# Two-layer conditioned trunk: the conditioning products in plain fp32 with weights stationary, and in a new order

## The reference

```
shift, scale, gate = split(silu(c) @ w_ada + b_ada, 3)        # w_ada: 1024 x 3072, per layer
h = rms_norm(x, norm_g) * (1 + scale) + shift                 # the same for ctx with c_ctx
(conv, glu, z, dq, dk, dv, dz, beta, decay, aq, ak, av, az, mgate) = split(h @ w_in)
y_conv  = silu(layer_norm(depthwise_conv(val * sigmoid(glu)))) * silu(z)
o_dn    = bidirectional gated delta rule over dq, dk, dv, beta, decay   (short convolutions before)
o_da    = differential softmax attention over aq, ak, av (4 heads, rotary positions)
x = x + gate * (sum_n sigmoid(mgate_n) * (y_n @ w_branch_n)) @ w_out
```

## Time and profile before

| | us |
|---|---|
| median of 3 runs | 1923.2 (1922.72 to 1926.9) |
| the profiled execution's own time | 1927.93 |
| span of its trace | 1926.1 |
| PE busy | 1799.3 (93%) |
| PE weight loads | 1497.2 (78%) |
| DVE busy | 1127.7 (59%) |
| ACT busy | 971.5 (50%) |
| POOL busy | 669.2 (35%) |

### The profile page before, as it was taken

How to read it: one execution, slowest core, us unless ns; L and a number is a source line. 1 busy time by engine, 2 the same in 40 slices (tenths; PEclk the granted TensorE clock), 3 DMA queues, 4 the chain that set the end, 5 groups by cost and what they waited for, 6 DMA issues and landing times. The chain is left out here.

```text
span 1926.1 us, 27717 instructions
## 1 busy us (share of the span) xinstructions
PE 1799.3 (93%) x11060; PEld 1497.2 (78%) x11060; DVE 1127.7 (59%) x1610; ACT 971.5 (50%) x1297; POOL 669.2 (35%) x490
## 2 busy tenths in 40 slices
PE   6789996899999999999999978999798999999999
PEld 5678886898888888888788857878696787777777
DVE  5556495459667656553234255749759866465343
ACT  6657523336445455553653156753337564555661
POOL 0011421537743434453153000144346544433150
PEclk9899998999999999999999999999799999999999
DMA  7123224422221122233244213324222221212352
GB/s 300 34 77 110 72 72 146 133 67 59 95 77 44 55 72 75 82 104 116 89 129 163 96 54 96 98 78 121 78 67 66 77 66 55 72 50 91 106 186 87
DMA packets 76414, 178.86 MB, mean 93 GB/s; under 512 B 6464, under 2 KB 29312, under 8 KB 76160
## 3 DMA queue, kind: packets, MB, share of 16 engines
q1 hardware_dynamic: 34272, 122.46, 20.6%
q10 hardware_dynamic: 42016, 54.63, 8.3%
HBM read 156.00 MB, written 21.07 MB: 92 GB/s over the span
## 5 line engine op out<-in xcount | busy, mean ns | idle before, releaser
L506 PE MATMUL banks<-hH,wHs 128*128 128x512 f32 x1984 | 599.0, 364 | 46.9 <-DVE hL L474 20.5
L506 PE MATMUL banks<-hH,wLs 128*128 128x512 f32 x1984 | 582.8, 355 | 0.0
L506 PE MATMUL banks<-hL,wHs 128*128 128x512 f32 x1984 | 581.1, 355 | 0.0
L1973 POOL TENSOR_TENSOR wLs<-raw,wHs 128x512 fp32r<-128x512 f32 x272 | 410.8, 1536 | 465.2 <-ACT wHs L872 465.2
L506 PEld LDWEIGHTS banks<-hH,wHs 128*128 128x128 f32 x1984 | 327.0, 191 | 123.6 <-issue 26.1
L506 PEld LDWEIGHTS banks<-hL,wHs 128*128 128x128 f32 x1984 | 324.8, 191 | 55.5 <-issue 2.2
L506 PEld LDWEIGHTS banks<-hH,wLs 128*128 128x128 f32 x1984 | 324.6, 191 | 54.7
L872 ACT ACTIVATE wHs<-raw 128x1024 fp32r<-128x1024 f32 x210 | 219.7, 1053 | 219.4 <-DMA raw<-wstream 219.2
L1529 DVE SCALAR_TENSOR_TENSOR acc<-padc,vecs,acc 128x783 f32<-128x783 f32 (+1 forms) x240 | 294.6, 1281 | 0.0
L861 ACT ACT_TABLE_LOAD x180 | 230.9, 1283 | 30.2 <-issue 13.0
L906 ACT ACTIVATE Pa<-banks,stat 128x768 f32<-128x768 f32 (+1 forms) x80 | 64.6, 813 | 144.0 <-DVE stat L1467 144.0
(11 more groups left out here) (242 smaller groups left out, 2330.8 us busy)
## 6 DMA issues: line engine op xcount, KB each, us to landing
raw<-wstream SPq DMA_DIRECT2D x210, 512.0 KB, 3.6
araw<-wstream SPq DMA_DIRECT2D x16, 512.0 KB, 12.6
E<-g_rows ACTq DMA_DIRECT2D x16, 384.0 KB, 7.0
egb<-eg_rows ACTq DMA_DIRECT2D x20, 256.0 KB, 4.2
inb<-intra_rows ACTq DMA_DIRECT2D x20, 256.0 KB, 4.5
parked_logits<-sg ACTq DMA_DIRECT2D x13, 384.0 KB, 4.1
xs<-xT SPq DMA_DIRECT2D x8, 384.0 KB, 11.4
intra_rows<-E ACTq DMA_DIRECT2D x8, 384.0 KB, 3.1
```

The lines of the kernel that those rows point to most:

```text
L506: last = pe.matmul(out[:, a:b], w, m[:, kt, a:b], start=(kt == 0 and j == 0), stop=(kt == kts - 1 and j == 2))
L1973: ins = pool.tensor_tensor(wL[w % RING][:, o:o + 512], raw[w % RING][:, o:o + 512], wH[w % RING][:, o:o + 512].bitcast(F32), ALU.subtract)
```

## The change

Pairs are now made with the raw weights, in plain fp32, as the loaded operand, and the two vectors as moving operand of two columns. The result stands in PSUM as columns, so that the split of weights and vectors, the copy to `adar`, the transposes and their waits go away. For the first eight pairs DVE adds the bias in one instruction (`first_col`) and makes the factor of the norm for two tiles after each second pair; for later pairs ACT adds the bias in two instructions of 128 x 2.

```diff
-                    out = product(pe, pair, 2 * P)
-                    pe.wait_ge(*done("csL"))
+                    out = product(pe, pair, 4)
+                    pe.wait_ge(*done("cs32"))
                     if first_ada(l, m):
-                        pe.wait_ge(*done("ahi", m))
-                        pe.wait_ge(*done("alo", m))
-                    for u in units_of(it):
-                        pe.wait_ge(*done("hi", u))
-                        pe.wait_ge(*done("lo", u))
-                    w = ada_pair(l, m)
-                    for kt in range(KT):
-                        for j in range(2):
-                            last = pe.matmul(out[:, 0:2 * P].rearrange("p (u c) -> p u c", u=2), csx[:, 4 * kt:4 * kt + P],
-                                             w[j][:, :, kt * P:(kt + 1) * P], start=(kt == 0 and j == 0),
-                                             stop=(kt == KT - 1 and j == 1))
+                        pe.wait_ge(*done("araw", 2 * m + 1))
+                        w = [araw[:, 2 * m + j, :] for j in range(2)]
+                    else:
+                        for u in units_of(it):
+                            pe.wait_ge(*done("raw", u))
+                        w = [raw[WIDX[u] % RING] for u in units_of(it)]
+                    for j in range(2):
+                        for kt in range(KT):
+                            last = pe.matmul(out[:, 2 * j:2 * j + 2], w[j][:, kt * P:(kt + 1) * P],
+                                             cs32[:, kt, :], start=(kt == 0), stop=(kt == KT - 1))
                     last.then_inc(*tick("pe", "pe", pair))
...
-                    act.activation(adar[0:4, :], place[pair][0:4, 0:2 * P], ACT.Copy).then_inc(*tick_read("act", pair))
+                    for j in range(2):
+                        act.activation(ada[:, l, 2 * m + j, :], place[pair][:, 2 * j:2 * j + 2], ACT.Identity,
+                                       bias=vecs[:, l, V_BADA + 2 * m + j:V_BADA + 2 * m + j + 1]).then_inc(
+                                           *tick_read("act", pair))
```

```diff
+FIRST_TILES = ((0, 1, 2), (3, 4, 5), (6, 7), (), (), (), (), ())
+FIRST_PAIR = (0, 4, 1, 5, 2, 6, 3, 7)
...
-    for t in range(KT):
-        out += [("ada", 0, t), ("nsum", 0, t)]
+    for v, t in enumerate(FIRST_TILES[:4]):
+        out += [("ada", 0, v)] + [("nsum", 0, i) for i in t]
+    out += [("ada", 0, 4), ("nh", 0, 0), ("ada", 0, 5), ("nh", 0, 1), ("nh", 0, 2), ("ada", 0, 6), ("ada", 0, 7), ("nh", 0, 3)]
     for l in range(DEPTH):
-        out += [("nh", l), ("gb", l)]
+        out += ([("ada", l, 10), ("ada", l, 11)] + [("nh", l, i) for i in range(4)] if l else []) + [("gb", l)]
...
-        late = [("ada", 0, m) for m in range(8, 12)] + [("ada", 1, m) for m in range(12)] if l == 0 else []
+        late = [("ada", 0, m) for m in range(8, 12)] + [("ada", 1, m) for m in range(10)] if l == 0 else []
```

More of the change, by code:

```diff
@@ L209, in low_on_vector @@
 def low_on_vector(u):
-    return u[0] in ("gb", "dk", "dv", "dq", "cz", "branch2", "branch0", "wout") or u[0] == "ada" and u[1] == 0
-FIRST = [("ada", 0, m) for m in range(2 * KT)]
+    return u[0] in ("gb", "dk", "dv", "dq", "cz", "branch2", "branch0", "wout")
+FIRST = [("ada", 0, 2 * m + j) for m in FIRST_PAIR for j in range(2)]
 ITEMS = schedule()
@@ L625, in _ @@
                 elif k == "gb":
+                    if l == 0:
+                        pe.wait_ge(*done("con_in"))
                     unit(units_of(it)[0], "gb")
@@ L831, in _ @@
             sp.dma_start(csb[:, :, :], cT).then_inc(*tick("c_in", "c_in", by=16))
-            for t in range(KT):
-                if t == 1:
+            for v, tiles in enumerate(FIRST_TILES):
+                for m in (2 * v, 2 * v + 1):
+                    sp.dma_start(araw[:, m, :], wstream[m]).then_inc(*tick("ada_raw%d" % v, "araw", m, by=16))
+                got[("araw", 2 * v)] = got[("araw", 2 * v + 1)]
+                if tiles:
+                    x = slice(tiles[0], tiles[-1] + 1)
+                    sp.dma_start(xs[:, x, :], xT[:, x, :]).then_inc(*tick("x_tiles%d" % v, "xt", tiles[0], by=16))
+                    for t in tiles:
+                        got[("xt", t)] = got[("xt", tiles[0])]
+                if v == 0:
                     sp.dma_start(cons[:, :], con).then_inc(*tick("small_in", "con_", by=16))
@@ L868, in ahead @@
                     v = UNITS[w]
+                    done_hi[0] += 1
+                    if v[0] == "ada":
+                        continue
                     act.wait_ge(*done("raw", v))
@@ L1004, in _ @@
                 elif k == "nh":
-                    for t in range(KT):
+                    if l == 0 and it[2] == 3:
+                        ahead(UNITS[0], 1)
+                    for t in (2 * it[2], 2 * it[2] + 1):
                         for p, (a, b) in enumerate(segs(TOK)):
@@ L1458, in maxes, with scales @@
+            def scales(l, tiles=slice(0, KT), last=KT - 1):
+                dve.wait_ge(*done("ada", l, last))
+                dve.scalar_tensor_tensor(gs[:, l, tiles, :], ada[:, l, 8 + tiles.start:8 + tiles.stop, :], 1.0,
+                                         bc(vecs[:, l, V_NG + tiles.start:V_NG + tiles.stop], 2), ALU.add,
+                                         ALU.mult).then_inc(*tick("dve", "gs", l, last))
             def maxes(l, h, qt):
@@ L1502, in low @@
                     done_lo[0] += 1
-                    if not low_on_vector(v):
+                    if v[0] == "ada" or not low_on_vector(v):
                         continue
@@ L1944, in _ @@
                     if t == 0:
+                        dve.wait_ge(*done("ada", l, 11))
                         low_m(l, KT - 2)
@@ L1991, in _ @@
                 stage[0], k, l = it[0], it[0], it[1]
-                if k == "ada":
-                    for u in units_of(it):
-                        ahead(u, ada_lead(l, it[2]))
-                    if l == 0 and it[2] == 6:
-                        ahead(UNITS[0])
-                elif k == "gb":
+                if k == "gb":
                     pool.wait_ge(*done("h", l, KT - 1))
```

145 lines of the change are left out of this document (28 added, 117 removed).

## The result

The changed kernel takes 1978.69 us (median of 4 runs, 1973.02 to 1989.8) against 1923.43 us for the kernel before in the runs beside it: the ratio is 1.03, interval 1.026 to 1.0341. It is slower, as forecast, but by 55 us and not by 29, and it lies outside the range of 1900 to 1966 us. The profiled execution took 1980.93 us; its span is 1979.1 us, 53.0 us more than before, and the two traces are compared on that.

A forecast was written before the change was run, and what follows sets the result against it. The prediction took PE to bound the kernel, busy 1799.3 of 1926.1 us. Start +2, solve +2, attention part +20 and border +5 made +29 us, 1952 on the median of 1923.2, stated as 1951; range 1900 to 1966, its own case 1932 to 1970.

The forecast's parts named there:

- The price of a pair: Each pair on PE: 32 loads at 0.11 us (full clock) or 0.17 (half), 3.5 or 5.4 us, against 2.19 before.
- The clock: PE during and behind pairs: the clock falls in most cases, each episode costing 2 us; six of eight attention pairs.
- Rival 1: Whole kernel: the clock holds at 2.4 GHz through the loads; -11 us, 1912; chance 0.31.
- Rival 2: Clock falls only at start, solve and border, the dense part recovers within the pair; +15 us, 1938; chance 0.12.
- rival 3: All pairs cheap, loads at the transposes' pace of 0.04 us, 1.3 us a pair; -39 us, 1884; chance 0.07.
- rival 4: Start: the change doesn't overlap the norm, so the full-clock gain there is gone; 1928; chance 0.05.
- The start: First eight pairs and norm of layer 0: PE becomes the late engine, gb ends at 75.2; +2 us.
- The solve: Solve of layer 0, six pairs at half clock: ends at 357.3, +4 us, +2 after egb's wait takes up some.
- The attention part: Dense PE stretch, eight pairs instead of ten, none hidden: own price, two pairs less and clock episodes; +20 us.
- The border: Between the layers: two pairs delay ACT's first hH, then hL and gb; +2.4 or +5 us, +5 in the sum.
- over 10: Sign at the border: ACT's first hH of layer 1 starts over 10 us behind the last sum, not 3.9.
- The sum: Whole kernel: +2 + 2 + 20 + 5 = +29 us, forecast 1951 us; chance 0.45.

The follow-up runs named there:

- x11: Changed kernel (two columns) with the first dz units split on ACT and POOL behind the solve's last two pairs: 1970.74 us, ratio 1.0242.
- x1: Changed kernel with gb of layer 1 split earlier at the border, on ACT and DVE during the norm: 1970.77 us, ratio 1.0238.
- x2: Changed kernel with 128 moving columns in each product of a pair instead of 2, same loads and order: 1933.41 us, ratio 1.0044.
- x9: Kernel before with only the new start, 128 columns moving, and gb's split there made earlier on ACT and DVE: 1911.22 us, ratio 0.9943.
- x7: Changed kernel with 128 moving columns, gb of layer 1 split earlier and the first dz units split behind the solve's last pairs: 1916.15 us, ratio 0.9975.
- x4: Changed kernel with the two border pairs moved back to the attention part of layer 0: 1968.07 us, ratio 1.0221.

## Why the direction was right and the size wrong

**The price of a pair** held at full clock: 3.63 us against 3.5, and the load pace 0.113 against 0.11. At half clock it failed. The prediction took 0.17 us a load, the distance of the first two loads after an idle time, although also had 0.22 for the load after them, which it kept as the upper end. A sustained stream goes at 0.20 (31.87 / 160): a pair is 6.4 us, not 5.4. The first distance of a stream was read as its pace.

**The clock** behaved as taken, with one difference: in the dense part most pairs still ran at 1.00, and the fall came behind them, behind six of the eight as forecast. Two windows of 4 us behind a pair of the changed kernel:

```profile
508.40:512.40 4.00, 4.00 (x24) 3.49 (x25) 3.41 (x4) 2.54 (x5) 1.38 (x1) 1.00 0.69 243
...
856.10:860.10 4.00, 4.00 (x17) 3.71 (x17) 1.93 (x3) 3.04 (x6) 2.76 (x3) 0.50 0.69 226
```

That the six came out exact is in part luck, as x11's three and x1's seven show. Rival 1, the clock that holds, is refuted for this kernel, and x2 shows that it was right about the loads themselves: with 128 columns moving the same stream of loads holds 1.00. Rival 2, a dense part that stays at full clock, is refuted by the same windows, rival 3 by the 0.113 us a load, and rival 4 by x2, whose start gained 11.1 us.

**The start** was forecast at +2 us and cost +6.7. The order of the work and the new bound, PE itself, were right; the sum failed by the half-clock pace. The last pair ended at 68.70 and not at 64.7: the five pairs took 31.87 us against 26.4, 5.5 more, and had begun 1.5 us earlier than forecast. The wait of 1.78 us for the first split was missing.

**The solve**, from its first pair to the scan, was forecast at +4 us and was +10.2 (310.76 to 368.40 against 305.45 to 352.86). Six pairs took 34.9 us against some 31.5, and the products between and behind them ran slow as well: the one between the last two pairs (L672) took 5.3 us where 3.0 had been put, and 4.1 us passed behind the last pair against 2.9; only the one behind the second pair was shorter, 4.5 us against 6.5. The prediction halved the clock for the pairs and not for all that stands between them. Of the 5.3 us wait for `egb` behind, 1 us came back (4.3 us remain), not 2.

**The attention part** was forecast at +20 us and measured +19.0, but not for the reasons given. x2 splits it: the clock costs 17.3 us (forecast 14), and the form itself +1.7 (forecast +6.1). In that +1.7 lie 6.3 us of the new wait for POOL, so that the total came out right is luck. "ACT, DVE and POOL lose their splits here (...), and that is worth nothing" was wrong on both sides. Something was gained: PE idled 5.3 of 420 us before and 0.84 in x2. And something was lost: the item of a pair was also the place where ACT and POOL split the next units ahead of time. With the item emptied, nobody did that ahead of the first products behind the scan, and PE waited 6.34 us for POOL:

```profile
434.44 6.18 POOL L1905 TENSOR_TENSOR wLs<-raw,wHs 128x512 fp32r<-128x512 f32 x5
437.06 0.98 PE L491 MATMUL banks<-hH,wHs 128*128 128x512 f32 x2 [6.34 <-POOL wLs L1905]
```

The prediction would have been wrong there with a clock of 1.00 behind the pairs, or with a pair under 2.2 us; the clock was 1.00 behind two of the eight only, and no pair was that short. Timeline of a pair, changed kernel:

```profile
852.09 4.08 PE L571 MATMUL banks<-cs,raw 128*128 128x2 f32 x32
...
858.07 0.99 PE L491 MATMUL banks<-hH,wHs 128*128 128x512 f32 x2
858.86 0.84 PE L491 MATMUL banks<-hL,wHs 128*128 128x512 f32 x2
```

The products behind that pair take 0.99 and 0.84 us where 0.51 is the full-clock value (third row of x9's timeline above). The 17.3 us are those of one trace: x11 and x7 have the same splits in this part and differ in the columns, and there it takes 769.3 and 764.5 us, so in x11's trace, with three falls of the clock, two columns cost 4.8 us.

**The border** was forecast at +5 us and cost +18.4; this is the largest miss, and the step of the prediction that failed is its path there: it took ACT's order to be all that makes the two pairs cost, and it gave the splits that ACT, DVE and POOL lose with the pairs no term. The prediction followed the wait of ACT for the pair results (6.21 us; the first `hH` starts 11.65 us after the start of `rsn`, L846, and "over 10" had been named) and `hH`, `hL`, `gb` behind it. It did not ask where the weights of `gb` are split. The ring of four buffers is full of the last two pairs when the norm begins, and the new items of a pair no longer split anything ahead. So `gb`'s split stands behind all eight tiles of the norm on both ACT and DVE, and PE, which before did `gb` tile by tile beside the norm, does all of it after. Before the change it began 6.59 us behind the last sum, and not 18.64 us behind the pairs:

```profile
1129.55 0.98 PE L506 MATMUL banks<-hH,wHs 128*128 128x512 f32 x2 [6.59 <-DVE hL L474]
```

x1 and x4 show it from two sides: an earlier split takes 7.5 us of the 18.4 off the border, no pairs there take 17.9 off, and PE waits the same 6.59 us as before. What is left in x1 is pairs and pair results, whose cost varies with the clock; in x7, where the clock holds and the split is early, the border costs +5.7.

**The sum.** Of the 24 us missing, 13.4 are the border's, 7.8 the solve's (the table's +9.8 against the +2 in the sum), 4.7 the start's; -1 us each come from the attention part and from the way to the solve. Sorted by cause through the experiments: 48 us of the span are the clock (x2, and 45 to 47 of the medians; the forecast held 40 for it, the distance between its +29 and the -11 of rival 1), 14 to 17 us the two late splits (x2 against x7: 1933.41 to 1916.15 is 17, and 14 when each is taken against the kernel before on its own chip), and without both the change is worth -6 us (x7). Rival 1's 1912 was, by x7's 1916, nearly the time of the same change with a clock that holds and splits in their place.

Left open: between 32 and 128 columns nothing was tried, so where the clock begins to hold everywhere isn't known, nor what in the engine makes the difference, nor why it falls behind some pairs of a dense part and not behind others.

## What to carry to other kernels

An operation that is bound by its loads looks fully busy in the profile and may still lower the clock of everything around it: read the granted clock over the operation, and try a wider moving operand that costs no time because the loads hide it. When an item is emptied, list what else rode on it; here it was the place where other engines prepared the next item's weights, and its loss cost about a third of what the clock's did. A step moved to a border must be followed through every buffer that it fills there, not only through the results that it delivers.

## What the runs showed of the hardware that was not expected

A longer instruction stream can be faster: 64 times the moving columns in 384 products, with the same loads, cost next to nothing in their own time (18.03 us for five pairs, and 3.63 for one with two columns at full clock) and gave back 45 us. A load of 128 x 128 in fp32 takes 0.113 us in a stream at 1.00 and 0.20 at 0.50, while the first two after an idle time can be 0.17 apart at 0.50. And the clock stayed low through most of 32 us in which PE was busy without a gap. Weight loads in the start, the changed kernel and then x2:

```profile
39.70 1.40 PEld L571 LDWEIGHTS banks<-cs,araw 128*128 128x128 f32 x6
```
```profile
39.87 0.86 PEld L571 LDWEIGHTS banks<-cs,araw 128*128 128x128 f32 x7
```

Six loads take 1.40 us in the first row, and seven take 0.86 us in the second.
